# Attention scores laid out with keys on partitions: the maximum and the sum over keys taken by GpSimd across partitions, the softmax denominator applied at the gate

## What is computed

```python
logits = jnp.einsum('bnqkgd,bnskd->bnkgqs', q, kb).astype(jnp.float32)
logits = logits * (1.0 / math.sqrt(HEAD_DIM)) + band_bias(rel_bias)[None, None]
...
m = jnp.maximum(jnp.max(logits, axis=-1, keepdims=True), sink)
p = jnp.exp(logits - m)
denom = jnp.sum(p, axis=-1, keepdims=True) + jnp.exp(sink - m)
p = (p / denom).astype(vb.dtype)
o = jnp.einsum('bnkgqs,bnskd->bnqkgd', p, vb)
```

## Time and profile before

| what | value |
|---|---|
| median of 3 runs (lowest, highest) | 1342.64 us (1342.61, 1342.78) |
| span of the profiled execution, first to last instruction | 1341.4 us |
| what the median has beyond that span | 1.2 us |
| units of the attention | 32, from 395.9 to 967.7 us, 17.87 us each |
| granted TensorE clock, mean over the span | 0.998 |

### The profile page before, as it was taken

One profiled execution on the slowest core, in us unless ns is written; L12 is line 12 of the kernel. 1 busy time (PEld: TensorE's weight loads), 2 busy tenths in 40 slices (PEclk: granted clock), 3 DMA queues, 4 the chain that ended last, 5 costly groups with the idle time before them and its releaser, 6 DMA issues.

```text
span 1341.4 us, 16542 instructions
## 1 busy us (share of the span) xinstructions
PE 1327.9 (99%) x6038; PEld 1098.0 (82%) x6038; DVE 916.2 (68%) x1140; ACT 540.6 (40%) x944; POOL 89.1 (7%) x151
## 2 busy tenths in 40 slices
PE   9999999999999999999999999999999999999997
PEld 8887788888888888888888888888888888888886
DVE  7899776324578459985589745998439896665376
ACT  7854632322233433434334343344323444322444
POOL 1222121000000000000000000000000221100001
PEclk9999999999999999999999999999999999999999
DMA  9779995988898998879987799788898978899778
GB/s 362 304 264 372 355 374 154 311 310 317 299 293 244 303 303 272 236 213 308 314 288 243 242 309 283 252 256 245 296 348 290 334 251 290 295 311 359 270 259 302
DMA packets 167888, 390.01 MB, mean 291 GB/s; under 512 B 77920, under 2 KB 90240, under 8 KB 146176
## 3 DMA queue, kind: packets, MB, share of 16 engines
q1 hardware_dynamic: 148272, 322.08, 71.7%
q0 software_dynamic: 18240, 62.92, 12.8%
q10 hardware_dynamic: 1296, 3.96, 0.8%
HBM read 294.18 MB, written 98.93 MB: 293 GB/s over the span
## 4 chain that ended last, share of the span: by engine, by line
PE 89%; DVE 6%; issue 2%; DMA 1%; ACT 1%; POOL 0%; SPq 0%; POOLq 0%; DVEq 0%; ACTq 0%
PE banks L2035 85%; PE banks L2064 1%; DVE x_main L1365 1%; PE banks L2076 1%; DVE w_ring L1352 1%; DMA x_park<-e 1%; PE banks L1995 1%; PE banks L2085 1%; PE banks L2086 1%; DMA z<-in_x_t_dram 1%; DVE raw L1450 0%; DVE z L1474 0%; DVE raw L1462 0%; DVE e L1510 0%; ACT x_main L1002 0%
## 5 line engine op out<-in xcount | busy, mean ns | idle before, releaser
L2035 PE MATMUL banks<-x_main,w_ring 128*128 128x512 f32 x2352 | 551.2, 391 | 1.9 <-DVE x_main L1365 1.2
L2035 PEld LDWEIGHTS banks<-x_main,w_ring 128*128 128x128 f32 x2352 | 437.5, 188 | 93.9 <-issue 3.6
L971 ACT ACTIVATE w_ring<-raw 128x1024 fp32r<-128x1024 f32 x223 | 235.5, 1056 | 544.0 <-PE banks L2035 536.2
L1352 DVE TENSOR_TENSOR w_ring<-raw,w_ring 128x1024 fp32r<-128x1024 f32 x223 | 272.7, 1223 | 214.4 <-ACT w_ring L971 213.0
L2035 PE MATMUL banks<-x_far,w_ring 128*128 128x512 f32 x1680 | 393.5, 391 | 0.1
L2035 PEld LDWEIGHTS banks<-x_far,w_ring 128*128 128x128 f32 x1680 | 312.9, 188 | 65.1 <-DVE e L1510 0.5
L2035 PE MATMUL banks<-w_ring,x_main 128*128 128x512 f32 (+1 forms) x1020 | 230.9, 387 | 0.3 <-DVE e L1510 0.3
L2035 PEld LDWEIGHTS banks<-w_ring,x_main 128*128 128x128 f32 x1020 | 189.8, 188 | 39.6 <-DVE e L1510 0.7
L506 POOL DMA_DIRECT2D x_park<-x_main x104 | 55.9, 538 | 1007.0 <-DVE x_main L1365 1006.9
L1002 ACT ACTIVATE x_main<-z 128x512 fp32r<-128x512 f32 x104 | 64.9, 624 | 110.9 <-issue 84.3
L1365 DVE TENSOR_TENSOR x_main<-z,x_main 128x512 fp32r<-128x512 f32 x104 | 71.1, 685 | 35.5 <-ACT x_main L1002 35.4
(11 more groups left out here) (163 smaller groups left out, 852.8 us busy)
## 6 DMA issues: line engine op xcount, KB each, us to landing
x_far<-x_park SPq DMA_DIRECT2D x84, 1024.0 KB, 6.5
x_main<-x_park SPq DMA_DIRECT2D x84, 1024.0 KB, 6.1
raw<-in_w_blocks_dram SPq DMA_DIRECT2D x127, 512.0 KB, 5.7
x_park<-x_main POOLq DMA_DIRECT2D x104, 512.0 KB, 5.9
q_cur<-qkv_park SPq DMA_DIRECT2D x64, 128.0 KB, 5.0
z<-mix_park SPq DMA_DIRECT2D x16, 512.0 KB, 7.6
z<-in_x_dram SPq DMA_DIRECT2D x6, 1024.0 KB, 12.8
x_park<-e POOLq DMA_DIRECT2D x8, 512.0 KB, 6.2
```

The lines of the kernel that those rows point to most:

```text
L971: act.activation(w_ring[:, n % NW, :, 0, :], raw[:, c, k:k + 2, :], ACT.Copy).then_inc(w_hi_ready, 1)
L1352: dve.tensor_tensor(w_ring[:, n % NW, :, 1, :], raw[:, c, k:k + 2, :], w_ring[:, n % NW, :, 0, :], ALU.subtract).then_inc(w_lo_ready, 1)
L2035: op = pe.matmul(bank, left, right, start=(first and i == 0), stop=(kt == HK - 1 and i == 2), skip_group_check=goes_on)
```

## The change

The scores are made with the roles of the operands swapped: two matmuls, keys on partitions and 8 heads x 64 queries in the free dimension, 512 columns in one bank. The bias is loaded in that layout. The maximum over keys is then one over partitions, and so is the sum of the exponentials. Both are made by GpSimd with a library instruction, `partition_all_reduce`, which leaves its result in all 128 partitions (`top` and `total`). The sink takes part as a second row of 512 columns beside the scores: VectorE takes the maximum with it, subtracts from both rows in one instruction, and one exponential on ScalarE covers both. The probabilities lie as the product with the values wants them, so that the four transposes go away. They are not divided; instead `total` is inverted and multiplied into the gate `g_cur` before `gate_output` uses it. The transpose of the values moves from the ninth quarter of a unit to its head.

```diff
+            def key_max(u):
+                pool.wait_ge(logits_read, u + 1)
+                if u > 0:
+                    pool.wait_ge(shift_step, 2 * u)
+                pool.partition_all_reduce(top, logits[u % 2][:, 0, :], P, bass.bass_isa.ReduceOp.max).then_inc(max_ready, 1)
+
+            def key_sum(u):
+                pool.wait_ge(exp_done, u + 1)
+                if u > 0:
+                    pool.wait_ge(weight_step, 3 * u)
+                pool.partition_all_reduce(total, probs[:, 0, :], P, bass.bass_isa.ReduceOp.add).then_inc(key_sum_ready, 1)
...
+                        if o == 1:
+                            key_max(u)
+                        elif o == 6:
+                            key_sum(u)
...
-                for j in range(PAIRS):
-                    op = act.activation(probs[:, j, :], logits[u % 2][:, j, :], ACT.Exp, bias=row_min[:, j:j + 1],
-                                        scale=-1.0, accum_out=row_sum[:, j:j + 1])
-                op.then_inc(exp_done, 1)
+                act.wait_ge(shift_step, 2 * u + 2)
+                act.activation(probs[:, :, :], probs[:, :, :], ACT.Exp).then_inc(exp_done, 1)
...
-                act.activation(pt_hi[:, :], pt_ps, ACT.Copy).then_inc(pt_hi_ready, 1)
+                act.activation(pt_hi[:, :], probs[:, 0, :], ACT.Copy).then_inc(pt_hi_ready, 1)
...
+            def scale_logits(u):
...
+                rows = slice(CHUNK if u < 2 else 0, P)
+                dve.scalar_tensor_tensor(out=logits[kv][rows, 0, :], in0=logit_ps[rows, :], scalar=SCALE,
+                                         in1=bias[rows, kv * PAIRS * 2:(kv + 1) * PAIRS * 2, :].rearrange("p h s -> p (h s)"),
                                          op0=ALU.mult, op1=ALU.add).then_inc(logits_read, 1)
...
+                dve.wait_ge(max_ready, u + 1)
+                dve.tensor_tensor(top, top, logits[kv][:, 1, :], ALU.max).then_inc(shift_step, 1)
+                dve.wait_ge(shift_step, 2 * u + 1)
...
+                dve.tensor_tensor(probs[:, :, :], logits[kv][:, :, :], top.unsqueeze(1).to_broadcast([P, 2, N]), ALU.subtract
+                                  ).then_inc(shift_step, 1)
...
+            def weight_gate(u):
+
+                dve.wait_ge(key_sum_ready, u + 1)
+                dve.tensor_tensor(total, total, probs[:, 1, :], ALU.add).then_inc(weight_step, 1)
+                dve.wait_ge(weight_step, 3 * u + 1)
+                dve.reciprocal(total, total).then_inc(weight_step, 1)
...
+                for par in range(2):
+                    rows = slice(par * HEAD, (par + 1) * HEAD)
+                    op = dve.tensor_tensor(g_cur[rows, :, :], g_cur[rows, :, :], total_by_half[rows, par, :, :], ALU.mult)
+                op.then_inc(weight_step, 1)
...
-                dve.tensor_tensor(pt_lo[:, :], pt_ps, pt_hi[:, :], ALU.subtract).then_inc(pt_lo_ready, 1)
+                dve.tensor_tensor(pt_lo[:, :], probs[:, 0, :], pt_hi[:, :], ALU.subtract).then_inc(pt_lo_ready, 1)
...
+                queries = q_cur[:, :, :].rearrange("p h s -> p (h s)")
+                pe.matmul(logit_ps, k_cur[:, 0, :], queries, start=True, stop=False)
+                pe.matmul(logit_ps, k_cur[:, 1, :], queries, start=False, stop=True).then_inc(qk_done, 1)
```

More of the change, by code:

```diff
@@ L312, in build @@
         zeros = sb("zeros", [P, CHUNK], X + 18 * KB + 1600)
[L314 to L325, removed]
+        bias = sb("bias", [P, HEADS, CHUNK], Z)
+        logits = [sb(f"logits{i}", [P, 2, N], Z + 4096 + 4096 * i) for i in range(KVH)]
+        probs = sb("probs", [P, 2, N], Z + 12288)
+        top = sb("top", [P, N], Z + 16384)
+        total = sb("total", [P, N], Z + 18432)
+        v_win = sb("v_win", [P, BAND], Z + 20480)
+        g_cur = sb("g_cur", [P, PAIRS, CHUNK], Z + 20992)
+        o_mix = sb("o_mix", [P, PAIRS, CHUNK], Z + 22016)
+        o_lo = sb("o_lo", [P, PAIRS, CHUNK], Z + 23040)
+        q_cur = sb("q_cur", [P, PAIRS * 2, CHUNK], Z + 24064, F32R)
+        k_cur = sb("k_cur", [P, 2, BAND], Z + 26112, F32R)
+        pt_hi = sb("pt_hi", [P, N], Z + 27136, F32R)
+        pt_lo = sb("pt_lo", [P, N], Z + 29184, F32R)
+        v_cur = sb("v_cur", [P, KVH, 2, HEAD], Z + 31232, F32R)
         u_buf = sb("u_buf", [P, 2, 2 + S], Z + 32 * KB - 32)
@@ L343, in build @@
         table_dump = small[:, 92:96]
-        row_min = small[:, 28:32]
-        row_sum = small[:, 32:36]
-        row_inv = small[:, 36:40]
         y_ssq = small[:, 40:48]
@@ L1237, in _ @@
                     elif 0 <= u < UNITS:
-                        if o == 3:
+                        if o == 2 and u % 2 == 0:
+                            turn_v(u // 2)
+                        elif o == 6:
                             exp_logits(u)
-                        elif o == 9:
-                            if u % 2 == 0:
-                                turn_v(u // 2)
-                            turn_p(u)
+                        elif o == 7:
+                            split_p(u)
                     if (n, quarter) in SCALE_FIRST_AT:
@@ L1773, in _ @@
                         if o == 1:
+                            scale_logits(u)
+                        elif o == 3 and u % 2 == 0:
+                            turn_v_lo(u // 2)
+                        elif o == 5:
                             shift_logits(u)
-                        elif o == 4:
-                            normalise(u)
+                        elif o == 8:
+                            split_p_lo(u)
                         elif o == 10:
-                            if u % 2 == 0:
-                                turn_v_lo(u // 2)
-                            turn_p_lo(u)
+                            weight_gate(u)
                     if o == 3 and 0 < u <= UNITS:
@@ L2060, in queries_by_keys, with turn_values @@
                 else:
[L2061 to L2077 removed]
+                    pe.wait_ge(logits_read, u)
+                queries = q_cur[:, :, :].rearrange("p h s -> p (h s)")
+                pe.matmul(logit_ps, k_cur[:, 0, :], queries, start=True, stop=False)
+                pe.matmul(logit_ps, k_cur[:, 1, :], queries, start=False, stop=True).then_inc(qk_done, 1)
+            def turn_values(chunk):
+                pe.wait_ge(v_loaded, chunk * 16 + 16)
+                if chunk > 0:
+                    pe.wait_ge(v_ready, chunk)
+                pe.transpose(v_ps[:, 0:P], v_win[:, :], ident[:, :]).then_inc(v_turned, 1)
             def probs_by_values(u):
```

102 lines of the change are left out of this document (39 added, 63 removed).

## The result

The changed kernel takes 1421.32 us, the one before 1342.71 us beside it: ratio 1.0585, 95% interval 1.0573 to 1.0597. It is slower by 5.9%, where 1499 us was forecast. The profiled execution's span is 1419.4 us.

The account below looks back on a forecast made before the run. TensorE's stream bounds the kernel before, VectorE sets the pace after. Span 1341.4 - 12.2 (TensorE) + 141.7 (heavy units) + 26.9 (light units) = 1497.8, plus 1.2 outside the span: 1499 us; range 1334 to 1660, about 0.8.

Parts of the forecast that it names:

- the likeliest case: Reductions stop VectorE's two-SBUF-input instructions throughout, T between 2.4 and 7.2 us: 1407 to 1691 us, chance 0.56.
- stopped in part: Rival: each reduction stops VectorE for one pass (1.2 us) only; 1364 us, between 1345 and 1400, chance 0.08.
- heavy units: The 18 of 32 units where VectorE works 15.7 us each; forecast 25.36 us each, 141.7 us over in all.
- TensorE's 0.38 us a unit: Four transposes gone (0.36 us), scores 0.02 us shorter: 12.2 us in all, a TensorE-bound unit becoming 17.49 us.
- light units: The other 14 units, VectorE working 9.3 us each; forecast 19.4 us each, 26.9 us over in all.
- VectorE's net 1.75 us: VectorE's list per unit: 2.93 us of instructions removed, 4.68 us added, before any stop by the reductions.
- The reciprocal: VectorE's inversion of the 128x512 total, priced like a TENSOR_SCALAR of that shape: 0.54 us.
- T: Time of one GpSimd reduction over partitions, taken as 4.2 us from three to four passes (3.6 to 4.8).
- The exclusion: VectorE instructions with two SBUF inputs stand still for all of each GpSimd reduction, less 0.5 us a heavy unit.
- the sign that VectorE is not stopped: `w_lo` on VectorE keeping at most 1.22 us while GpSimd is busy; then 1336 us, that rival's chance 0.22.
- What is late next: In the units, `w_lo` uses up its two steps of lead in two units, then TensorE waits for it.
- T = 62 us: If the library reduction resembled the skill's `tensor_reduce` along partitions, a quarter of 247,699 ns: some 5,050 us in all.

Follow-up runs that it names:

- e1: Changed kernel with the reciprocal of 128x512 replaced by a multiplication by 1.0 of the same shape (output not the reference's): 1370.3 us, ratio 1.0208.
- e6: Kernel before plus one reciprocal of 128x512 per unit on VectorE, on a tile nobody else reads: 1368.6 us, ratio 1.0194.
- e5: Changed kernel with both reductions replaced by a memset and the reciprocal by a multiplication by 1.0 (output not the reference's): 1332.9 us, ratio 0.9921.
- e2: Changed kernel, computing the same, with sum and sink's part gathered into a compact tile and the reciprocal over 128x256: 1386.1 us, ratio 1.0323.
- e3: Changed kernel with both GpSimd reductions over partitions replaced by a memset of the same tile (output not the reference's): 1377.9 us, ratio 1.0264.

## Why the prediction was right, and where not

- **The time, in part by luck.** 1421.3 us lies in the range of the likeliest case, 1407 to 1691, but that case's mechanism (VectorE stopped for the whole of each reduction) is not what ran. e1 is the kernel with that place of the list at 0.43 us, near the 0.54 that was priced, and with the reductions as they are: 1370.3 us, near the 1364 of the rival "stopped in part" and outside the likeliest case. What carried the time into it was 2.8 us for the reciprocal that the prediction had not priced.
- **The bound and its turn.** Right: TensorE's stream bounds the kernel before, VectorE the heavy units after (98% busy), and the sign follows. e6 shows it cleanest: 3.34 us more on VectorE, for whose result no other engine waits, cost 26 us.
- **TensorE's 0.38 us a unit.** Right in the main: 12.2 us forecast, 9.8 us seen in e5. There the light units run at 17.3 us, better than the 17.49, since the matmuls behind the transposes are quicker too, and the heavy ones at 17.7.
- **VectorE's net 1.75 us without surprises.** Right: VectorE's busy time in e5 is 51.4 us above before, 1.61 us a unit, and with 0.43 in place of 0.54 for the reciprocal 1.64 was priced. It falls differently than thought, 1.2 us in a heavy unit and 2.2 in a light one by the windows.
- **The reciprocal.** A step that failed. I priced it at 0.54 us from two instructions of four elements, 171 and 170 ns. It takes 3.35 us at 512 columns and 1.75 at 256 (e2): the difference is 6.25 ns a column. At four columns that is 25 ns beside some 146 ns that do not grow. The TENSOR_SCALAR (170 ns at four columns, 427 at 512 in e1) grows by 0.5 ns a column, so its fixed part is some 168 ns, and the two differ by about as much as the rate adds: their meeting at 170 was chance. Two tiny shapes cannot exclude a rate. The Trainium skill's remark on the iterated divide ("VectorE: DVE Perf Modes", "First, the fixed hardware budget"), against which I weighed the rows, was the better guide: 4.3 us by the estimate from it, 3.35 measured. It cost 51 us (e1), where the net loss is 78.6.
- **The reductions' length.** T was put at 4.2 us, from three to four passes. Alone they take 1.78 (maximum) and 3.23 us (sum), the sum 1.8 times the maximum; with their waiting 2.70 and 3.65. The means, 2.5 and 3.2, are both below the 3.6 to 4.8 within which the prediction called its T right.
- **The exclusion.** The other step that failed: right in kind, wrong in size. The prediction held VectorE for all of T. Shown: 2.10 us of the sum's 3.23, 0.88 of the maximum's 1.78; on average 0.98 us a reduction by e3, less than 2.10 and 0.88 would give, since a reduction also meets instructions that are not lengthened, such as the sum out of PSUM at 602.21, or an idle VectorE. The rule of the Trainium skill ("SBUF — State Buffer", "Who interferes with whom"), that the two exclude each other for the whole instruction, holds for the earlier trace rows, and does not hold for this library instruction, which lets go before it ends. The rival "stopped in part" had the mechanism; its price of 34 us compares with 43 measured (e3).
- **Who stands for whom.** The prediction let the `w_lo` behind the scores stand for all of the maximum, and named a `w_lo` that keeps its 1.22 us as the sign that VectorE is not stopped. It keeps them, 1223 ns, and yet VectorE is stopped: the `w_lo` starts first (601.07 against 601.25), the maximum waits for it (24 of the 32 show 2.68 us in place of 1.78), and what comes next is held. The sign was a wrong one.
- **The sum, corrected.** Heavy unit: 25.4 forecast, less 5.9 (held 2.0 in place of 7.9), plus 2.8 (the reciprocal), makes 22.3; measured 22.3. That this meets to a tenth is in part chance: VectorE's 16.9 in e5, with 2.9 for the reciprocal and 2.0 held, makes 21.8, its busy time in the changed kernel, and the other 0.5 us it is idle. Two errors of opposite sign left the forecast 78 us too high.
- **The light units.** 19.4 forecast, 18.0 measured. With 2 us held in place of 8.4 and 2.8 more for the reciprocal the sum is about 15.8 us (16.1 measured busy), under TensorE's 17.5. Against e5's light units the 14 take 9.2 us more: 3.7 us TensorE is idle, nearly all in the one wait for ScalarE above, and 5.5 us are longer matmul time, at a mean granted clock of 0.97 to 0.98 in three of the four stretches.
- **What is late next.** I named `w_lo`. It is `pt_lo` (37.9 us) and the sums that free PSUM banks (18.6 us); `w_lo` has 1.6. It has two steps of lead, and `pt_lo` has not; that this is the reason is argued and not tested.
- **The clock.** Not in the sum. Of 89.7 us between e5 and the changed kernel, 32.1 are longer matmul time, with part of the stretch granted 1.2 GHz in place of 2.4. It goes with the waits: e5, with few of them, has a mean granted clock of 0.999, the changed kernel 0.977.
- **One sum of the prediction.** With T = 62 us its own sum gives 1499 + 64 x 57.7, about 5,190 us, and not 5,050. Nothing else rests on it.

## What to carry to other kernels

Look at the busiest windows, not at the mean share: an engine that is 68% busy over the span had only 2.2 us of room in each of 18 units, and once that was used each microsecond put on its list there came out as time. Price an instruction's rate only from a shape of its own size; from a tiny one take nothing but the fixed part. Work moved to an idle engine can still cost time on another: here each reduction on GpSimd lengthened VectorE's instructions by 0.98 us.

## What the runs showed of the hardware that I had not expected

- VectorE's reciprocal costs 6.25 ns a column (3.35 us at 128x512, 1.75 at 128x256, float32); a multiplication by a constant at 128x512 takes 0.43 us (e1).
- `partition_all_reduce` at 128x512: 1.78 us for a maximum, 3.23 for a sum, and it holds VectorE's instructions on SBUF off for the first 0.88 and 2.10 us only. It waits itself for such an instruction that is under way, and then shows 2.68 and 4.30 us in the changed kernel.
- An instruction with one SBUF input is held too: the TENSOR_SCALAR of 128x512 (L1675) takes 1.00 us on average in the changed kernel, 0.59 without the reductions (e3), and 0.54 before. Beside that tile it reads two columns of constants.
